# A gather of expert rows for a PEER layer: U and v of an expert side by side in HBM, some gathers bringing both

## The reference

```python
q = (xb @ w_q).reshape(PEER_BLOCK, PEER_HEADS, 2, PEER_HALF)
s = jnp.einsum('thpd,hpnd->thpn', q, sub_keys)
sv, si = lax.top_k(s, PEER_TOPK)
...
fs, fi = lax.top_k(cand, PEER_TOPK)
experts = jnp.take_along_axis(cidx, fi, axis=-1)
g = jax.nn.softmax(fs, axis=-1)
hid = jax.nn.gelu(jnp.einsum('td,thkd->thk', xb, u[experts]))
return jnp.einsum('thk,thkd->td', g * hid, v[experts])
```

## Time and profile before

| | us |
|---|---|
| median of 3 runs | 3815.91 (3809.19 to 3816.87) |
| profiled execution, first to last instruction | 3884.6 |
| PE, DVE, ACT, POOL busy in it | 2398.7, 2918.6, 531.0, 2400.6 |
| DMA | 1295.78 MB, mean 334 GB/s |
| eidx of lane 0 of phase 0, then of lane 3 of phases 0 to 3 | 443.4; 719.9, 1618.2, 2494.3, 3393.3 |

### The profile page before, as it was taken

How to read it: one execution, slowest core, us unless ns; L and a number is a source line. 1 busy time by engine, 2 the same in 40 slices (tenths; PEclk the granted TensorE clock), 3 DMA queues, 4 the chain that set the end, 5 groups by cost and what they waited for, 6 DMA issues and landing times. The chain is left out here.

```text
span 3884.6 us, 29311 instructions
## 1 busy us (share of the span) xinstructions
PE 2398.7 (62%) x8928; PEld 1667.0 (43%) x8928; DVE 2918.6 (75%) x5647; ACT 531.0 (14%) x1237; POOL 2400.6 (62%) x2052
## 2 busy tenths in 40 slices
PE   8899527786698718667598717687788815600000
PEld 6677412464585413345486413355576513200000
DVE  2311796787877896788888796688777797799889
ACT  2310101122210101112110101122210101100000
POOL 0000377766566576767576577776566577777776
PEclk9889769897798859988699859998789857955555
DMA  4334599999799989999899989999899998999998
GB/s 154 108 103 139 206 336 361 379 366 382 279 402 409 345 312 359 367 409 392 318 388 409 363 313 359 367 393 376 291 363 409 369 344 301 356 352 382 356 374 352
DMA packets 359900, 1295.78 MB, mean 334 GB/s; under 512 B 40512, under 2 KB 40768, under 8 KB 359744
## 3 DMA queue, kind: packets, MB, share of 16 engines
q0 software_dynamic: 294912, 1073.87, 73.0%
q1 hardware_dynamic: 64256, 217.94, 14.9%
q10 hardware_dynamic: 576, 2.10, 0.1%
HBM read 1291.65 MB, written 2.10 MB: 333 GB/s over the span
## 5 line engine op out<-in xcount | busy, mean ns | idle before, releaser
L1057 POOL DMA_INDIRECT ring<-in_peer_u,eidx x1024 | 1213.0, 1185 | 956.1 <-DVE eidx L1181 478.1
L1057 POOL DMA_INDIRECT ring<-in_peer_v,eidx x1024 | 1187.4, 1160 | 507.3 <-issue 291.4
L1094 DVE CUSTOM_DVE_ANT_0 ring<-ring,hp 128x1024 f32<-128x1024 f32 x1024 | 1236.2, 1225 | 236.3 <-DMA ring<-in_peer_u,eidx 207.3
L1099 DVE SCALAR_TENSOR_TENSOR acc<-ring,wgt,acc 128x1024 f32<-128x1024 f32 x744 | 952.0, 1288 | 86.8 <-DMA ring<-in_peer_v,eidx 62.8
L519 PE MATMUL bank<-xt,panel 128*128 128x256 f32 x4096 | 952.5, 392 | 42.3 <-issue 16.5
L519 PEld LDWEIGHTS bank<-xt,panel 128*128 128x128 f32 x4096 | 803.3, 198 | 173.8 <-issue 42.1
L752 PE MATMUL bank<-ring,dg 128*128 128x512 f32 x1120 | 541.2, 625 | 486.3 <-ACT dg L826 344.9
L752 PEld LDWEIGHTS bank<-ring,dg 128*128 128x128 f32 x1120 | 207.4, 197 | 807.1 <-issue 610.8
L594 PE MATMUL bank<-dg,ex 128*128 128x128 f32 x640 | 114.8, 354 | 146.1 <-DVE dg L1341 71.2
L594 PEld LDWEIGHTS bank<-dg,ex 128*128 128x128 f32 x640 | 107.7, 262 | 157.8 <-issue 141.6
L1329 DVE TENSOR_REDUCE nmax<-bank 128x1 f32<-128x128 f32 (+3 forms) x128 | 62.2, 486 | 150.7 <-PE bank L573 134.1
(11 more groups left out here) (164 smaller groups left out, 1908.7 us busy)
## 6 DMA issues: line engine op xcount, KB each, us to landing
panel<-in_panels SPq DMA_DIRECT2D x368, 512.0 KB
ring<-in_peer_u,eidx POOLq DMA_INDIRECT x1024
ring<-in_peer_v,eidx POOLq DMA_INDIRECT x1024
work<-in_rel_bias SPq DMA_DIRECT2D x16, 512.0 KB
gb<-in_ln_g SPq DMA_DIRECT2D x8, 512.0 KB
gb<-in_ln_b SPq DMA_DIRECT2D x8, 512.0 KB
panel<-in_keys SPq DMA_DIRECT2D x16, 256.0 KB
work<-in_x SPq DMA_DIRECT2D x4, 512.0 KB, 5.4
```

Of the source, the lines that this page charges most:

```text
L1057: pool.indirect_dma_start(ring[:, n % RING, :], None, t_in["peer_u" if kind == "U" else "peer_v"], bass.IndirectOffsetOnAxis(ap=eidx[:, t, ...
L1094: v.tensor_tensor_reduce(row, row, hp[:, t, :], 1.0, 0.0, ALU.mult, ALU.add, hid[:, t, c:c + 1]).then_inc(used, 1)
L1099: stt(out=acc[:, t, :], in0=row, scalar=wgt[:, t, c:c + 1], in1=acc[:, t, :], op0=ALU.mult, op1=ALU.add).then_inc(used, 1)
```

## The change

In HBM the arrays U and v become one array `peer`: row e holds U of expert e and behind it v of expert e, 8 KB. A new kind of item, "P" (pair), is one gather that brings both rows into two neighbouring slots of `ring`. Heads 0 to 2 of phases 0 to 2 and all heads of phase 3 are pairs; heads 3 to 7 of phases 0 to 2 stay single gathers of 4 KB per token, which see the same array as twice as many 4 KB rows (index 2e for U, 2e+1 for v). So a phase from 0 to 2 has 96 pairs and 320 singles, phase 3 has 256 pairs, and the program issues 1504 gathers in place of 2048. Each lane from T1 to T3 takes the 32 pairs of one head; the mixers of the next phase take 256 singles (before 280), keys L and T0 64 as before; the tail is 160 pairs.

Of a pair, DVE does the U half as before. For each k, once both tiles are done, ACT takes gelu of the two columns, waits for that, scales by the gates (two one-column copies), waits again, and writes two diagonals; PE sums both v halves. No v half of a pair is summed on DVE. Singles follow the old way, with v on PE for every second k of T0 alone. `acc` is no longer opened by a scaling: the first `add_sums` of a phase fuses ALPHA times `hp` with the banks. In phase 3 that addition moves behind the tail. `ring` has 16 slots, there are 7 panel buffers, `xn` shares memory with `pt`, and in phase 0 the load of the second half of x moves from the A loads to ahead of the O loads, behind a wait for `yc_ev`.

```diff
-RING = 15
-PANELS = 6
+RING = 16
+PANELS = 7
...
+PAIR_HEADS = LANES - 1
+
+def stream(s):
+
+    def pairs(head):
+        return [("P", head, k, t) for k in range(TOP) for t in range(TILES)]
...
+    rows = []
+    for head in range(HEADS if s == PHASES - 1 else PAIR_HEADS):
+        rows += pairs(head)
+    if s == PHASES - 1:
+        return rows
+    rows += u_rows(PAIR_HEADS) + u_rows(PAIR_HEADS + 1)
+    for head in range(PAIR_HEADS + 2, HEADS):
         for v, u in zip(v_rows(head - 2), u_rows(head)):
             rows += [v, u]
...
-LANE_ROWS = (0, 40, 64, 64)
-MIXER_ROWS = {"A": (16, 60), "B": (8, 32), "C": (12, 56), "G": (16, 64), "O": 16}
+LANE_PAIRS = TOP * TILES
+MIXER_ROWS = {"A": (16, 60), "B": (8, 24), "C": (12, 40), "G": (16, 64), "O": 16}
...
-    return kind == "V" and stage == "T" and (it > 1 or it == 0 and k % 2 == 1)
+    return kind == "P" or kind == "V" and stage == "T" and k % 2 == 1
...
+            for key in TAIL:
+                sums(key)
...
             def gelus(key):
...
+                    if kind == "P" and t == TILES - 1:
+                        g = PAIR_GROUP[n]
+                        act.wait_ge(used, DVE_PLACE[n] + 1)
+                        fn(ge[:, :, c:c + 1], hid[:, :, c:c + 1], ACT.Gelu_apprx_tanh).then_inc(pair_gelu, 1)
+                        if k == 0:
+                            act.wait_ge(gates_done, p * LANES + head // 2 + 1)
+                        act.wait_ge(pair_gelu, g + 1)
+                        for i in range(TILES):
+                            ins = fn(wgt[:, i, c:c + 1], ge[:, i, c:c + 1], ACT.Copy, scale=gate[:, i, c:c + 1])
+                        ins.then_inc(pair_wgt, 1)
+                        act.wait_ge(pair_wgt, g + 1)
+                        for i in range(TILES):
+                            diagonal(n + 1 - TILES + i, i, c)
...
+                for old, summed in OLD[n]:
+                    if summed and old in PE_PLACE:
                         pool.wait_ge(pe_used, PE_PLACE[old] + 1)
                     else:
                         pool.wait_ge(used, DVE_PLACE[old] + 1)
                 c = head * TOP + k
+                slot = SLOT[n]
+                if kind == "P":
+                    pool.indirect_dma_start(ring[:, slot:slot + 2, :].rearrange("p a b -> p (a b)"), None, t_in["peer"],
+                                            bass.IndirectOffsetOnAxis(ap=eidx[:, 0, t, c:c + 1], axis=0)
+                                            ).then_inc(row_in[slot], 16)
+                else:
+                    which = 0 if kind == "U" else 1
+                    pool.indirect_dma_start(ring[:, slot, :], None, one_row,
+                                            bass.IndirectOffsetOnAxis(ap=eidx[:, which, t, c:c + 1], axis=0)
+                                            ).then_inc(row_in[slot], 16)
...
-                        if head == 0:
-                            for i in range(TILES):
-                                ts(acc[:, i, :], hp[:, i, :], ALPHA, None, ALU.mult).then_inc(acc_open, 1)
-                            dve.wait_ge(acc_open, (p + 1) * TILES)
...
+                        if group % 2:
+                            ins = tt(part, part, pa[t * 2 + half][:, :], ALU.add)
+                        else:
+                            ins = stt(out=part, in0=hp[:, t, cols], scalar=ALPHA, in1=pa[t * 2 + half][:, :],
+                                      op0=ALU.mult, op1=ALU.add)
...
+                    if paired(s, it * 2 + hh):
+                        ins = ts(eidx[:, 0, :, cols], ef[:, pairs, :], base, None, ALU.add)
+                    else:
+                        for which in range(2):
+                            ins = ts(eidx[:, which, :, cols], ef[:, pairs, :], 2.0, 2.0 * base + which, ALU.mult, ALU.add)
```

More of the change, by code:

```diff
@@ L137, in row_plan @@
         for it in range(1, LANES):
-            plan += [((s, "T", it, i), k) for i, k in enumerate(spread(LANE_ROWS[it], CHOICES))]
-    left = ROWS - sum(LANE_ROWS)
+            plan += [((s, "T", it, i), TILES * k) for i, k in enumerate(spread(LANE_PAIRS // TILES, CHOICES))]
+    left = len(ITEMS) - sum(k for _, k in plan)
     plan += [((PHASES, "Z", i, 0), k) for i, k in enumerate(spread(left, left // 8))]
@@ L493, in _ @@
                 for stage in "CGO":
+                    if s == 0 and stage == "O":
+                        sp.wait_ge(yc_ev, 2)
+                        load_x(1)
                     for i in range(STAGE_PANELS[stage]):
@@ L817, in gelus @@
                 for n in rows_of(key):
[L818 to L826, removed]
+                    p, kind, head, k, t = ITEMS[n]
+                    c = head * TOP + k
+                    if kind == "V" and n in PE_PLACE:
+                        act.wait_ge(wgt_ready, single_heads(p, head) + 1)
+                        diagonal(n, t, c)
                     if kind == "U" and k == TOP - 1 and t == TILES - 1:
@@ L830, in gelus, with diagonal @@
                         fn(ge[:, :, cols], hid[:, :, cols], ACT.Gelu_apprx_tanh).then_inc(gelu_done, 1)
+                    if kind == "P" and t == TILES - 1:
[11 more added lines that the diff above has]
+                            diagonal(n + 1 - TILES + i, i, c)
+            def diagonal(n, t, c):
+                i = PE_PLACE[n]
+                if i >= DIAGS:
+                    act.wait_ge(pe_used, i - DIAGS + 1)
+                fn(dg[:, i % DIAGS, :], ident, ACT.Copy, scale=wgt[:, t, c:c + 1]).then_inc(diags, 1)
             def take_turned(dst, banks, turned, taken, base):
@@ L1109, in add_sums @@
                     for half in range(2):
-                        part = acc[:, t, half * 512:(half + 1) * 512]
-                        ins = tt(part, part, pa[t * 2 + half][:, :], ALU.add)
+                        cols = slice(half * 512, (half + 1) * 512)
+                        part = acc[:, t, cols]
+                        if group % 2:
[3 more added lines that the diff above has]
+                                      op0=ALU.mult, op1=ALU.add)
                 ins.then_inc(added, 1)
@@ L1455, in finish @@
             def finish(p):
-                dve.wait_ge(used, max(last_sum.values()) + 1)
                 if p < PHASES - 1:
```

105 lines of the change are left out of this document (57 added, 48 removed).

## The result

The changed kernel takes **3711.63 us** at the median (3709.99 to 3712.2, 4 runs), the kernel before 3812.55 beside it (3802.9 to 3816.87): a ratio of 0.9716, 95% interval 0.9682 to 0.975. It is 2.8% faster; forecast were 3744 us and 1.9%.

A forecast was written before the change was run, and what follows sets the result against it. POOL's gather issue and DVE together were taken to bound the tail, with DVE on stage C's chain; tail -67, lanes +66, mixers -72, small edits 0 made -73, 3811.6 us profiled, scaled to 3744 us; range 3690 to 3800.

The forecast's parts named there:

- Tail, -67: Tail: 160 pairs replace 344 gathers, the DMA sets the pace at 2.56 us a pair; 424 us against 491.
- PE's price: Tail: PE takes two matmuls per pair, 0.94 us each at the 0.5 clock, 0.44 at full.
- rival 1: Pairs hold ring slots too long; at a turn of 23 us, net +94, 3908 us; chance 0.11.
- Lanes, +66: Lanes: more row blocks, DMA binds, 19 us idle at query stops and lane ends; +15 in phases 1-3, +21 in 0.
- Mixers, -72: Mixers: 24 fewer row blocks on DVE, 16 from stage C, 8 from B; 24 us saved in each of three phases.
- My sign for C: Stage C: ACT's 54.8 us wait for DVE's maxima was to become some 15 us shorter.
- Small edits, 0: Dropped scalings, added index writes, sixteenth slot, seventh panel buffer and SP's new wait: each taken as 0.
- The scaling: Whole kernel: 3811.6 us in a profile times 3815.91 / 3884.6, the profile being 1.8% above the median.
- rival 4: All goes well: ring covers gaps, mixers give 31 us each; -178, 3641 us; chance 0.15.
- 2: Rival: gathers never hold 409 GB/s; at 363 a pair costs 2.89 us, net +105, 3919 us; chance 0.04.
- 5: Rival: single U gathers slow with rows 8 KB apart; at twice the time net +173, 3986 us; chance 0.03.
- Rival 3: Mixers don't shorten, DVE's freed time becomes a wait for PE; 3815 us, no change; chance 0.10.

The follow-up runs named there:

- a1: Changed kernel with each pair fetched by two 4 KB gathers into the same two slots: 3869.81 us, ratio 0.9958.
- b3: Kernel before with the tail's 172 v rows summed on PE through diagonals, single gathers as before: 3935.06 us, ratio 1.0067.
- b4: Kernel before, unchanged, measured a third time, on a chip where its median is 3822.42 us: 3819.95 us, profile span 3818.1.
- a3: Changed kernel with 14 ring slots (7 pairs) for 16: two executions took 3799 and 3811 us, two 8477 and 11947.
- b1: Kernel before with the changed dealing of rows alone, no pairs: 3923.84 us, ratio 1.0074.
- a2: Changed kernel with 6 panel buffers for 7: 3703.05 us, ratio 0.9683.
- b5: Kernel before with 16 ring slots for 15 and 5 panel buffers for 6: 3885.84 us, ratio 0.9978.
- b2: Kernel before with U and v side by side in HBM, every gather still a single 4 KB row: 3896.61 us, ratio 1.0014.
- b0: Kernel before, unchanged, profiled again on a chip where its median was 3894 us: span 3887.9 us.

## Why the prediction was right or wrong, point by point

**What binds.** Right. POOL set the pace of the tail and, in the main, of the lanes before: in the tail 102.1 us of gaps named "issue" are all that POOL ever waits, on the faster chip too; in phase 1's lanes they are 51.8 us and all other waits 23. I had named DVE as its partner, on the ground that it is busy 441 of 491 us. It is a partner, but not by being full: a1 and b3 have DVE at 44% of the tail and POOL still sets the pace. DVE lengthens the gathers that begin while it works on a row. A gather with its gap would take 0.94 + 0.31 = 1.25 us, under the DMA's 1.28; it is the lengthened ones that bring the mean to 1.41. No run took DVE's part away by itself. In the changed kernel's tail half of the 152 gathers take 0.94 us and half 1.66, and both are under the 2.49 us that the DMA takes for a pair.

**Tail, -67.** Right in sign and kind; -76 against the profile that I used, -53 against b4, whose chip ran the kernel before about as fast as the first measurement did. Two errors meet. The pair costs 2.49 us, not 2.56, since an 8 KB packet passes at 421 GB/s: 154 x 2.49 + 29 = 412, against 415 measured. And the 491 us of before were, as I take it, a slower chip's; in b4 it is 468. The steady state shows itself in the timeline (start, us, instruction), one k of two tiles every 4.97 us (3449.79, 3454.76 and so on for the second tile's U half):

```profile
3451.05 0.21 ACT L869 ACTIVATE ge<-hid 128x2 f32<-128x2 f32 x1 [3.54 <-DVE hid L1150]
3451.29 0.48 ACT L874 ACTIVATE wgt<-ge,gate 128x1 f32<-128x1 f32 x2
3451.80 0.69 ACT L885 ACTIVATE dg<-cst,wgt 128x128 f32<-128x128 f32 x2
3452.13 0.93 POOL L1112 DMA_INDIRECT ring<-in_peer,eidx  x1 [0.31 <-issue]
3452.26 1.23 DVE L1150 CUSTOM_DVE_ANT_0 ring<-ring,hp 128x1024 f32<-128x1024 f32 x1 [1.25 <-DMA ring<-in_peer,eidx]
...
3452.35 3.67 PE L789 MATMUL bank<-ring,dg 128*128 128x512 f32 x8 [1.31 <-ACT dg L885]
...
3454.76 1.22 DVE L1150 CUSTOM_DVE_ANT_0 ring<-ring,hp 128x1024 f32<-128x1024 f32 x1 [1.26 <-DMA ring<-in_peer,eidx]
...
3455.08 1.71 POOL L1112 DMA_INDIRECT ring<-in_peer,eidx  x1 [2.02 <-PE bank L789]
```

Here POOL waits for PE to free slots and DVE waits for data. The two kinds of gather are here too: the one of 3452.13 began before DVE's instruction and took 0.93 us; the one of 3455.08 began within the instruction that ends at 3455.98, and ended at 3456.79. The waits of the tail:

```profile
ACT ge L869 <- DVE hid L1150: 278.6, 80, 6.4
DVE ring L1150 <- DMA ring<-in_peer,eidx: 196.5, 154, 2.9
POOL ring L1112 <- PE bank L789: 148.2, 72, 9.9
...
POOL ring L1112 <- issue: 34.8, 77, 2.9
```

That PE is named as the one that POOL waits for does not make it the bound: with two slots fewer the tail stayed (a3), and with two more too (412).

**PE's price.** Wrong by half. I read x4 in the earlier trace rows as two rows of two matmuls; four records are one v row. The page has 2464 records for 616 diagonals:

```profile
L789 PE MATMUL bank<-ring,dg 128*128 128x512 f32 x2464 | 1150.5, 616 | 440.8 <-ACT dg L885 417.0
...
L885 ACT ACTIVATE dg<-cst,wgt 128x128 f32<-128x128 f32 x616 | 212.9, 394 | 90.9 <-DVE wgt L1144 57.7
```

A v half takes 1.8 us, not 0.88, at full clock, and the 3.75 us that I halved are the price of one row at the 0.5 clock. At that clock PE, with 3.75 us a pair, would have been slower than the DMA and would have set the tail's pace. That it didn't is luck, as far as my argument goes: the granted clock was 0.98 in the tail with PE 71% busy, and 1.8 is under 2.49. The margin of rival 1 hung on it too: it was thinner than I wrote. The end behind the last landing took 21 us where I had 22, but PE's part of it was 3.67 us, not 1.9, as one k of two v halves is left, and the other parts were shorter:

```profile
3691.63 3.67 PE L789 MATMUL bank<-ring,dg 128*128 128x512 f32 x8 [1.26 <-ACT dg L885]
...
3695.34 2.48 DVE L1171 SCALAR_TENSOR_TENSOR acc<-hp,bank 128x512 f32<-128x512 f32 x4 [5.04 <-PE bank L789]
```

**Lanes, +66.** Right in sign, too high: +24 against b4 (+8, +7, +3, +6), +16 against the profile that I used. The term that was mis-sized is the time of DMA plus idle: 102 x 2.49 = 254 in place of 261, and of 286 us that leaves 286 - 254 - 11 - 7 = 14 us of idle DMA, not 19. That the idle time is the ring's to cover is shown: 14, 16 and 18 slots gave some 297, 285 and 276 us, and without idle the same sum is 272. Where it lies is seen in the windows of phase 1's lanes: behind the first query stop (queries from 1346 to 1362 us), behind a lane end (DVE without rows from 1402 to 1412), behind the second query stop (1441 to 1457) and behind the next lane end.

```profile
1362.00:1368.00 6.00, 5.63 (x13) 2.58 (x14) 1.44 (x4) 4.44 (x17) 1.97 (x2) 1.00 0.89 300
...
1414.00:1426.00 12.00, 10.14 (x20) 4.52 (x21) 12.00 (x49) 4.49 (x17) 4.39 (x4) 0.77 0.66 256
1456.00:1468.00 12.00, 11.55 (x33) 5.46 (x32) 3.44 (x6) 5.51 (x21) 5.01 (x5) 1.00 0.82 286
1508.00:1520.00 12.00, 9.53 (x17) 4.24 (x18) 12.00 (x45) 4.15 (x15) 3.46 (x3) 0.70 0.67 260
```

Against the share of 1.01 that the pairs have in between, some 4 us are lost behind each lane end, as forecast, but only 1 and 2 us behind the queries, where I had 4 to 5. Another 2 us are lost between 1320 and 1332 us, behind the LayerNorm that DVE makes there (1309 to 1314 us). No run took one of the stops away.

**Mixers, -72.** Right, and in C by its own reason: -86 against b4, of which stage C has 18, 22 and 19 and A and B 7, 7 and 5. b1, with the dealing alone, shows C's 18 us as clean as the changed kernel does. It doesn't show a gain for B in phases 1 and 3; a2 shows that the seventh panel buffer isn't the source of the 5 to 7 us in A and B, and b5 that a sixteenth slot gives the kernel before nothing there; the source stays open. My sign for C was wrong: ACT's wait for DVE's maxima is still 55 us in C (54.8 in the earlier trace rows). That the rows went from between these waits, and so left them as they were, is argued.

**Small edits, 0.** Right for all but the slot: a2 shows the seventh panel buffer at nothing, b2 the layout with eight more index writes a phase at 1.0014 (0.9988 to 1.004). The sixteenth slot is nothing to single gathers (b5), but I had put it at 0 for pairs too, and there it makes the eighth pair: a3, with seven, is 65 to 76 us slower, some two fifths of the 175 us that the change is worth on that chip. The new wait of SP was not tried alone; the start is 436 to 444 us with and without it.

**The scaling.** I took the profile's 1.8% over the median as a factor. If it is the difference between chips that b0 and b4 show, it is no factor: of their 70 us the tail has 36, the lanes 9, the mixers 19 and the start 6, while the changed kernel differs by 23 us between chips in all. Steps read from a slower chip's profile then overstate what the change gains on the other chip: the tail shrank by 53 us there, not by 76 or by the 66 (67 x 0.982) of my forecast.

**The sum.** I had -67 + 66 - 72 = -73 and got -53, +24 and -86 against b4, which with the start's +6 are -108; at the medians I forecast 72 us less and it was 101 less. Nearly all of what the sum missed is the lanes, 42 us too high; the tail's and the mixers' errors, 14 us each, cancel. That they cancel is luck. Against the very profile that I summed from, the change is -175, next to the -178 of rival 4.

**Rivals.** 1 falls by a3 for the tail, 2 by the 421 GB/s, 5 by b2. Rival 3 did not come, as the mixers shortened. Rival 4 came in part: the mixers gave 29 us a phase, between my 24 and its 31, and the lanes were nearer to its "no idle" than to mine.

## What to carry to other kernels

Where a gather's issue, not its bytes, sets the pace, put what is read together side by side and fetch it with one index: the same bytes cost half the issues. An engine that is half idle can still lengthen the issue; look at how long the single gathers take while it works and while it doesn't. The same change made by moving rows between stages, or from VectorE to TensorE, without the wider gather was slower here (1.0074 and 1.0067). And size the ring by the longest stop of whatever frees it, in time of transfer, before giving memory to prefetch that nothing waits for.

## What the runs showed of the hardware that I had not expected

- Gathers of 8 KB a row move at 421 GB/s, gathers of 4 KB a row at 409 at most. GpSimd's issue of an indirect gather takes the same time for either: 0.94 us at best and 1.0 to 1.3 on average.
- A gather's issue that begins while VectorE works on a 128x1024 row (U or v) nearly always ends 0.81 us after that instruction, however much of it was left; otherwise it takes 0.94 us. In the changed kernel's tail 76 of 152 are of the first kind, 1.66 us on average (b3 and a1: 1.26 and 1.23).
- A float32 matmul of 128x128 by 128x512 stands in the trace as two records of 0.46 us at full clock (3.67 us for the eight of two v halves).
- The kernel before differs by 1.9 to 2.5% between chips (3812 and 3822 against 3894 to 3909), half of it in the tail (36 of 70 us); the changed kernel by 0.6%.
- Two of four executions of the kernel with 14 slots took two and three times as long. It stays open why.
